# Compression with reordered copies and a split prompt unit, and packed query columns in the recurrence's small levels

## The reference

```python
ch = kp.reshape(B, n_ch, CMP_STRIDE, NSA_KV_HEADS, HEAD_DIM)
w1r = w1.reshape(CMP_RATIO, CMP_STRIDE, HEAD_DIM, CMP_HIDDEN)
parts = jnp.einsum('bnsgd,rsdh->rbngh', ch, w1r)
h = parts[0, :, 0:n_cmp] + parts[1, :, 1:1 + n_cmp]
out = jax.nn.gelu(h + (pe.reshape(-1) @ w1) + b1) @ w2 + b2
```

```python
att = jnp.einsum('bhtk,bhtsk,bhsk->bhts', qc, decay, kc)   # decay = exp(b_t - b_s), s <= t
o = o + jnp.einsum('bhts,bhsv->bhtv', att, vc)
```

## Time and profile before

| what | value |
|---|---|
| runs, median (lowest to highest) | 2225.09 us (2222.95 to 2227.34) |
| profiled execution, its own time | 2226.52 us |
| its span | 2224.7 us |
| mean granted TensorE clock, share of full | 0.974 |
| TensorE busy, share of the span | 95% |
| VectorE, ScalarE, GpSimd busy | 51%, 36%, 40% |
| compression, 186 to 442 us: TensorE busy, clock | 239.50 us of 256.00, 0.97 |
| recurrence, 986 to 1080 us: TensorE busy, clock | 77.15 us of 94.00, 0.87 |
| the same: VectorE and ScalarE busy | 80.84 and 62.46 us |

### The profile page before, as it was taken

How to read it: one execution, slowest core, us unless ns; L and a number is a source line. 1 busy time by engine, 2 the same in 40 slices (tenths; PEclk the granted TensorE clock), 3 DMA queues, 4 the chain that set the end, 5 groups by cost and what they waited for, 6 DMA issues and landing times. The chain is left out here.

```text
span 2224.7 us, 38518 instructions
## 1 busy us (share of the span) xinstructions
PE 2108.2 (95%) x15606; PEld 1881.6 (85%) x15606; DVE 1145.7 (51%) x2132; ACT 793.7 (36%) x1654; POOL 880.8 (40%) x631
## 2 busy tenths in 40 slices
PE   5998999999999999998899999999999999999998
PEld 3997888856777689987899999678999999997886
DVE  5116545355676710258530054666865665654558
ACT  3203222234655611336412221234333333333553
POOL 2322121011111131211211223364388788776785
PEclk9999999988999999998899999999999999999999
DMA  7564534283100051100322130321244434357762
GB/s 267 193 214 160 183 121 152 92 304 139 32 32 11 1 143 39 39 9 3 99 76 57 47 125 4 117 95 41 86 162 151 139 132 166 129 182 284 266 226 105
DMA packets 152760, 268.23 MB, mean 121 GB/s; under 512 B 17817, under 2 KB 86348, under 8 KB 147975
## 3 DMA queue, kind: packets, MB, share of 16 engines
q1 hardware_dynamic: 144375, 222.70, 30.0%
q0 software_dynamic: 8208, 43.07, 5.5%
HBM read 211.93 MB, written 58.08 MB: 121 GB/s over the span
## 5 line engine op out<-in xcount | busy, mean ns | idle before, releaser
L3518 PE MATMUL PS<-down_parts 128*128 128x512 f32 x924 | 211.7, 390 | 1.1 <-DVE down_parts L4091 1.1
L3518 PEld LDWEIGHTS PS<-down_parts 128*128 128x128 f32 x924 | 173.1, 188 | 38.7 <-issue 2.0
L3475 PE MATMUL PS<-part_hi,w_ring 128*128 128x258 f32 x1152 | 192.3, 285 | 0.0
L3475 PEld LDWEIGHTS PS<-part_hi,w_ring 128*128 128x128 f32 x1152 | 162.1, 191 | 4.3 <-issue 4.3
L3475 PE MATMUL PS<-sum_blocks,w_ring 128*128 128x258 f32 x1296 | 161.6, 285 | 1.9 <-DVE out_sums L4041 1.9
L3475 PEld LDWEIGHTS PS<-sum_blocks,w_ring 128*128 128x128 f32 x1296 | 159.7, 192 | 2.1 <-DVE out_sums L4041 2.1
L651 POOL TENSOR_TENSOR w_merge_parts<-w_merge_raw,w_merge_parts 128x1024 fp32r<-128x1024 f32 x24 | 59.3, 2496 | 202.4 <-ACT w_merge_parts L644 183.6
L3867 POOL TENSOR_TENSOR down_parts<-down_raw,down_parts 128x512 fp32r<-128x512 f32 x71 | 118.5, 1686 | 43.2 <-ACT down_parts L3673 42.9
L2399 PE MATMUL PS<-h_hi,w_merge_parts 128*128 128x344 f32 x768 | 131.9, 324 | 0.0
L2399 PEld LDWEIGHTS PS<-h_hi,w_merge_parts 128*128 128x128 f32 x768 | 122.5, 189 | 3.1 <-issue 3.0
L1865 ACT ACTIVATE scores<-scores,mins_p 128x640 f32<-128x640 f32 (+5 forms) x192 | 112.5, 589 | 25.2 <-DVE mins_p L1907 24.4
(11 more groups left out here) (617 smaller groups left out, 5182.9 us busy)
## 6 DMA issues: line engine op xcount, KB each, us to landing
down_raw<-act_blocks SPq DMA_DIRECT2D x77, 256.0 KB, 3.4
w_or_ada<-w_ada SPq DMA_DIRECT2D x8, 2048.0 KB
w_raw<-w_up SPq DMA_DIRECT2D x11, 1024.0 KB, 9.4
w_raw<-w_gate SPq DMA_DIRECT2D x11, 1024.0 KB, 6.7
w_down_rows<-w_down SPq DMA_DIRECT2D x11, 1024.0 KB, 7.3
w_down_blocks<-w_down_sums SPq DMA_DIRECT2D x11, 1024.0 KB, 8.7
down_raw<-w_down_blocks SPq DMA_DIRECT2D x44, 256.0 KB, 4.0
act_blocks<-act_sums SPq DMA_DIRECT2D x10, 1024.0 KB, 5.1
```

Source lines behind the costliest of these rows:

```text
L3475: last = pe.matmul(out[:, c, :], r32(w[:, k, :]), r32(h[:, k, QUART * c:QUART * c + QUART]), start=first and k + i == 0, stop=k == 3 and i ...
L3518: last = pe.matmul(PS[:, t, c], r32(s[:, x, P * (t % 4):P * (t % 4) + P]), r32(s[:, y, c]), start=first and i == 0, stop=last_j and i == 2 ...
```

## The change

In compression, ScalarE's and VectorE's work on a unit's second half is moved behind the copies of the first item of the unit after the next. ScalarE's old loop body is cut in two functions, `middle` (middle copy and late rows) and `gelu`. On TensorE the second item of the unit behind a prompt unit is transposed between the two halves of the prompt unit's first layer.

In the recurrence, for w = 3 to 6, the matmuls take only the query columns of second halves as moving operand (64 per tile), so eight tiles fill one PSUM bank. The mask is stored packed for these levels, and the pick reads PSUM and mask densely; its destination `att` keeps its stride.

```diff
     lev = [(s // (2 * h) == t // (2 * h)) & (s % (2 * h) < h) & (t % (2 * h) >= h) for h in (64, 32, 16, 8, 4, 2, 1)]
-    lev = [lev[0] | lev[1] | lev[2]] + lev[3:] + [s == t]
-    c["c_levels"] = np.stack(lev, 1).astype(np.int32)
+    small = [x.reshape(P, -1, 2, h)[:, :, 1].reshape(P, P // 2) for x, h in zip(lev[3:], (8, 4, 2, 1))]
+    c["c_levels"] = np.concatenate([lev[0] | lev[1] | lev[2], s == t] + small, 1).astype(np.int32)
...
                 for hh in range(2):
                     col = slice(P * hh, P * hh + P)
+                    if hh and u in FIRST:
+                        transposes(pe, items[units[u + 1][2][1]])
...
                 if u + 1 < NU:
-                    for k in units[u + 1][2]:
+                    for k in units[u + 1][2][:1 if u in FIRST else 2]:
                         transposes(pe, items[k])
...
-            u = 0
             for k in read_chunks(act, 0, even_read):
-                if u + 1 < NU and k == units[u + 1][2][-1]:
-                    gelu(u)
-                    u += 1
-            gelu(u)
+                u = items[k][0]
+                if u >= 2 and k == units[u][2][0]:
+                    gelu(u - 2, 1)
+                if u and k == units[u][2][-1]:
+                    middle(u - 1, 0)
+                    gelu(u - 1, 0)
+                    middle(u - 1, 1)
+            gelu(NU - 2, 1)
+            middle(NU - 1, 0)
+            gelu(NU - 1, 0)
+            middle(NU - 1, 1)
+            gelu(NU - 1, 1)
...
             for k in read_chunks(v, 1, odd_read):
                 u = items[k][0]
+                if u >= 2 and k == units[u][2][0]:
+                    sums(u - 2, 1)
+                    if u >= 3:
+                        out(u - 3)
                 if k == units[u][2][-1]:
...
                     if u:
-                        for hh in range(2):
-                            sums(u - 1, hh)
+                        sums(u - 1, 0)
                         late(u - 1)
-                    if u >= 2:
-                        out(u - 2)
+            sums(NU - 2, 1)
+            out(NU - 3)
...
                             out = PS[:, 2 * (U % 2) + c // 4, P * (c % 4):P * (c % 4) + P]
+                            if 3 <= w < 7:
+                                out = PS[:, 2 * (U % 2), HALFC * c:HALFC * c + HALFC].rearrange("p (n s) -> p n s", s=64 >> w)
...
                             else:
-                                last = pe.matmul(out, X[:, n % 3, cc], X[:, n % 3, cc], start=True, stop=True)
+                                last = pe.matmul(out, X[:, n % 3, cc], pair_halves(X[:, n % 3, cc], w)[1], start=True, stop=True)
...
                 elif w < 7:
-                    d, level, src = (t.rearrange("p c (n x s) -> p c n x s", x=2, s=64 >> w)[:, :, :, 1] for t in (d, level, src))
+                    d = d.rearrange("p c (n x s) -> p c n x s", x=2, s=64 >> w)[:, :, :, 1]
+                    level = lev[:, 2 * P + HALFC * (w - 3):2 * P + HALFC * (w - 2)].rearrange("p (n s) -> p n s", s=64 >> w).unsqueeze(1).to_broadcast([P, NT, HALFC // (64 >> w), 64 >> w])
+                    src = PS[:, 2 * (U % 2), :].rearrange("p (c n s) -> p c n s", c=NT, s=64 >> w)
```

More of the change, by code:

```diff
@@ L1252, in _, with middle @@
         def _(act):
-            def gelu(u):
+            def middle(u, hh):
+                act.wait_ge(l1_done, 2 * u + hh + 1)
+                if u:
+                    act.wait_ge(summed, 2 * (u - 1) + hh + 1)
+                if units[u][1] is not None:
+                    act.activation(m2[:, 2 * N3 * hh:2 * N3 * hh + 2 * N3], PS[:, 3, 0:2 * N3], ACT.Copy, scale=0.5).then_inc(m2_read, 1)
+                if u in late_at and hh == late_half(u):
+                    n = late_at.index(u)
+                    act.wait_ge(wa_done, n + 1)
+                    if n:
+                        act.wait_ge(wa_back, n)
+                    act.activation(arow[:, :], PS[:, 7, :], ACT.Copy).then_inc(wa_read, 1)
@@ L1254, in gelu @@
+            def gelu(u, hh):
                 which = units[u][0]
                 nb, c, nc_ = shape(u)
-                for hh in range(2):
[L1257 to L1271, removed]
@@ L1272, in _ @@
-            u = 0
-            for k in read_chunks(act, 0, even_read):
-                if u + 1 < NU and k == units[u + 1][2][-1]:
-                    gelu(u)
-                    u += 1
-            gelu(u)
+                act.wait_ge(summed, 2 * u + hh + 1)
+                act.wait_ge(hb_ready, 2 * which + hh + 1)
+                act.activation(H[:, u % 2, hh, 0:2 * nb * nc_], H[:, u % 2, hh, 0:2 * nb * nc_], ACT.Gelu_apprx_tanh,
+                               bias=hb[:, which, hh:hh + 1]).then_inc(gelu_done, 1)
@@ L2229, in hgrn_and_merge @@
         KdT = at("KdT", [P, NT, P], 59552)
-        lev = at("levels", [P, LEV - 1, P], 139104, I32)
+        lev = at("levels", [P, 4 * P], 139104, I32)
         Sd = at("S_dec", [P, 2, NB, DV], 18592)
@@ L2238, in hgrn_and_merge @@
         block = st.enter_context(nc.Block())
+        HALFC = P // 2
         jobs = 9 * HH
@@ L2288, in load_state @@
                 sp.dma_start(Sd[:, h % 2], a["state_hgrn"][0, :, h].rearrange("b k v -> k b v")).then_inc((s_in0, s_in1)[h % 2], 16)
-            sp.dma_start(lev[:, :, :], a["c_levels"][:, :, :]).then_inc(lev_in, 16)
+            sp.dma_start(lev[:, :], a["c_levels"][:, :]).then_inc(lev_in, 16)
             state(0)
@@ L2430, in _ @@
                             elif w == 6:
-                                last = pe.matmul(out, kk[:, h, cc], X[:, n % 3, cc], start=True, stop=True)
+                                last = pe.matmul(out, kk[:, h, cc], pair_halves(X[:, n % 3, cc], w)[1], start=True, stop=True)
                             else:
-                                last = pe.matmul(out, X[:, n % 3, cc], X[:, n % 3, cc], start=True, stop=True)
+                                last = pe.matmul(out, X[:, n % 3, cc], pair_halves(X[:, n % 3, cc], w)[1], start=True, stop=True)
                         last.then_inc(job_done, 1)
@@ L2661, in pick @@
                 src = PS[:, 2 * (U % 2):2 * (U % 2) + 2, :].rearrange("p a (c n) -> p (a c) n", n=P)
-                d, level = att[:, h % 2, :, :], lev[:, u, :].unsqueeze(1).to_broadcast([P, NT, P])
+                d = att[:, h % 2, :, :]
+                x = P if w == 7 else 0
+                level = lev[:, x:x + P].unsqueeze(1).to_broadcast([P, NT, P])
                 if w == 2:
```

## The result

The changed kernel takes **2269.64 us** (median of five runs, 2268.07 to 2284.57), the kernel before 2225.09 (five runs, 2222.24 to 2227.34). The ratio is 1.0214, with an interval of 1.0181 to 1.0248: it is slower by about 44.5 us. The forecast was 2252.5, with a range of 2233 to 2272: the median lies near its upper end, one of the five runs beyond it. By the ratio the loss is 47.6 us, which would be 2272.7. The direction and the compression came out as reckoned; the recurrence cost some 20 us where 2 were taken.

What follows compares the result with a forecast made beforehand. TensorE, 95% busy, was taken as the bound, losing time only to waits or a low clock. Steady stretches 14.4, prompt units 4.2, clock 6.8 and recurrence 2 made 27.4 us; 2225.1 + 27.4 = 2252.5 us, range 2233 to 2272.

Steps and rivals of the forecast that it cites:

- Steady stretches: Compression, four stretches of raw-item transposes: postponed sums and GELU delay ScalarE's group 4 copy; 3.6 us each, 14.4 in all.
- the third sum held by GpSimd: Steady compression stretches: VectorE's third sum collides with GpSimd's difference and stretches to over 1 us; collision term 0.9 us each.
- ScalarE's wait: Sign in the four steady compression stretches: ScalarE stands 1 to 3 us before a GELU between two items' copies.
- the wait before group 7: Sign in the steady compression stretches: TensorE waits some 3 us for ScalarE's copy before turning the last group.
- Prompt units: Compression, split first layers of keys' and values' prompt units: 2.5 us won is waited away behind VectorE; +2.1 each, 4.2 together.
- Clock in compression: Compression: new TensorE waits drop its clock four times, three steady and one prompt, 1.7 us each; 6.8 us.
- Recurrence: Recurrence, levels 3 to 6: narrow passes may let the clock fall once in head 0; +2 us, bounds -6.3 to +28.
- rival D: Recurrence: the clock collapses, +10 to +28 us instead of +2, giving 2260 to 2279 us; chance 0.1.
- The row at 417: Compression, L1081 at 417.33 us: 3.61 us in the cold after narrow passes, taken as showing they do not hold the clock.
- Pass length: Recurrence, levels 3 to 6: weight load sets the pace, so 64 columns instead of 128 gain 1.0 us at most.
- rival A: Recurrence: packed columns halve the pass, about -7 us; with compression's loss still slower, 2243 us; chance 0.05.
- Picks: Recurrence, picks of levels 5 and 6: they shorten, but VectorE's wait before them grows; worth 0, 5.3 us if on the path.

Runs made afterwards that it cites:

- e7: Kernel before with ScalarE's new compression order only (GELU between two items' copies), VectorE's sums still before its copies, no prompt split: 2222.72 us, ratio 0.9997.
- e5: Kernel before with ScalarE's and VectorE's new compression orders, without the split of the prompt units; recurrence as before: 2252.46 us, ratio 1.0119.
- e6: Kernel before with only the split of the prompt units, copies and sums in the old order: 2227.39 us, ratio 1.0015.
- e10: Kernel before with the packed 64-column recurrence plus unused 128-column filler matmuls ahead of levels 0 and 1: 2241.19 us, ratio 1.0075.
- e4: Kernel before with 64-column matmuls in levels 3 to 6, written to their old places, mask and pick as before: 2249.07 us, ratio 1.0128.
- e8: Kernel before, still 128 columns, with unused 128-column filler matmuls ahead of levels 0 and 1 in the recurrence: 2220.76 us, ratio 0.9988.

## Why the prediction was right and where it failed

**Steady stretches: right.** 14.4 us were forecast. The four stretches from the first transpose to L1081 take 9.12, 9.58, 9.11 and 9.12 us, 36.93 in all; before 4 x 5.53 = 22.12. That is +14.8. Each link is in the rows: the third sum held by GpSimd (1.15 us), ScalarE's wait (3.04, forecast as 1 to 3), the wait before group 7 (3.49, "some 3"). e7 against e5 shows that it is VectorE's order, the sums behind the copies, as the working had it, and not the GELU. The Trainium skill (SBUF — State Buffer, "SBUF: two separate sides") says that a VectorE operation with two SBUF inputs and a GpSimd one that reads SBUF lock each other out for a whole instruction; the trace agrees, since the sum ends 0.24 us behind GpSimd's difference.

**Prompt units: right in kind, a little low.** Forecast 2.1 us each. For the keys' one the next pair layer starts at 213.48 us, against 211.38 in the trace of before: +2.1. For the values', from the first transpose behind the last keys' unit to the start of the pair layer it is 25.5 us (327.27 to 352.79), where it was 22.4 (314.40 to 336.81): +3.1, with the transposes now at the low clock. e6 shows that the 2.5 us won are waited away.

**Clock in compression: near.** Forecast 6.8. L1081 loses 13.75 - 4 x 1.92 = 6.1 us in four falls, where three were counted, and the first-layer block behind it 1.0 more; in the first-layer block behind the values' prompt unit it is +1.2, behind the keys' -0.6. The fall at 417 is gone and gives 1.7 back, which the change did not cause: in all eleven other traces the same second-layer and late matmuls and the same wait of 0.38 us stand before L1081 there, and it takes 1.92 or 1.93 us. That makes 6.0. The sum 14.8 + 5.2 + 6.0 = 26.0 is the delay at the last L1088 of the compression, 467.23 against 441.25 us; forecast 25.4. Up to the recurrence's start 1.5 us come back (1010.5 - 986.0 = 24.5). That it fits this closely is partly luck: in the six traces with compression as before the recurrence starts between 981.3 and 989.2 us.

**Recurrence: the step that failed.** "In head 0 the levels stand apart, and halved they may let it fall once; later heads have full-width chunk matmuls between. I take +2 us." The mechanism was the one named (the clock with narrow passes), its size was taken wrong: it is +20.5, and rival D, at 0.1, is what happened. Two things in the step were wrong. It counted new falls, and there is one, in head 0, as it said; but 38 of the 48 us more at half clock are in heads 2 and 3, where the clock fell before the change as well, and where the packed levels now keep it down until the diagonal job. An engine at half speed for 48 us more loses at most half of it, 24 us, near the 20.5 measured. And the full-width chunk matmuls between the levels, which were to protect the later heads, do not: they stand between levels at 0.50, in the changed kernel and in e10. That the clock of before falls four times in the recurrence, twice ahead of a level 3 in or behind which it comes back, could have been read beforehand. The row at 417, on which the step rested, was weak ground: the same sequence keeps its clock in the eleven other traces, so that it pointed the right way is in part luck. The upper bound (+28, all levels cold) was in the sum, and should have carried much more than a tenth. The rule of the Trainium skill that was weighed there (TensorE: Matmul & The Clock Gate, "What's actually happening": the gate follows how busy PE was) would have made the term 0. Measured, TensorE was busy in the whole of every 1 us window from 1042 to 1057 in e10, with the clock at 0.50; the measurement decides.

**Pass length: right.** A narrow pass is hardly faster (2.00 and 1.97 us for sixteen, against 1.95 to 2.05), so rival A is out. The same page of the Trainium skill, "LDWEIGHTS (loading the stationary operand)", has the load of P columns at about P/1.2 ns, by which 128 would take an estimated 107 ns; at the full clock the trace agrees, with 0.107 to 0.111 us a pass for 9, 64 or 128 moving columns.

**Picks: half right.** They were worth nothing, as taken. "The picks of levels 5 and 6 shorten" was wrong but for 0.05 us: 1.30 to 1.32 us, against 1.36.

**What stays open.** Why e10 keeps the clock in its second head and loses it for 17 and 24 us in the third and fourth, with the same operations in each, is not settled, nor whether a single packed level would lose it, nor whether it is the number of the columns or the gaps between them. Half clock and lengths come from one trace of each kernel. After the recurrence 45.0 us of delay shrink to 43.1 at the end of the span; where the 1.9 are regained was not followed, nor where the 1.5 between compression and recurrence.

## What to carry to other kernels

Before moving work behind a shared copy, write down when the copy that the critical engine waits for will end: here one order of operations on VectorE cost 28 us, and the same idea on ScalarE alone cost nothing. Do not thin a matmul whose pace the weight load sets: it gets no shorter, and the half-empty stream can cost the clock, or keep it down where it had come back before. When one row shows a state change after a certain kind of work, look whether it recurs where the same work stands again, and price it by how often and for how long, not as a single event.

## What the runs showed of the hardware

- Passes of 128 weight columns with 64 moving ones ran with the clock at 0.50 although TensorE and its loads were busy in the whole of each 1 us window from 1042 to 1057 (e10); 128 moving columns in the same places kept 1.00 (58.0 against 6.8 us at half clock, with the same filler).
- Behind the same waits of 1.41 and 1.39 us the clock fell with either width. With 128 columns it came back after 10 and 7 us, in or right behind level 3; with 64 after 27 and 28 us, in the diagonal job.
- The same narrow matmuls and wait before L1081 cost the clock in one trace of twelve (3.61 us, against 1.92 or 1.93).
- A predicated copy of 128x512 takes 1.30 to 1.36 us when it writes runs of one or two columns and 0.70 to 0.73 with runs of four, whether source and mask are dense or strided. With a dense destination 128x1024 take 1.31.
- With narrow passes the longer executions are those with the lower mean clock: in e4 2241.84, 2244.89, 2253.25 and 2257.18 us go with 0.970, 0.966, 0.961 and 0.958.
- Keeping the clock up where TensorE also waits for VectorE won nothing that shows: e8 has 6.8 us at half clock in a recurrence of 115.3 us, e5 20.5 in 114.9.
